# Adding four tiles' squares on VectorE at stage boundaries, with the weight split moved behind the residual in two parts

## The reference

```python
def rmsnorm(x, g):
    y = xf * lax.rsqrt(jnp.mean(xf * xf, axis=-1, keepdims=True) + RMS_EPS)
    return (y * g.astype(jnp.float32)).astype(x.dtype)
...
    m = c_act @ w + b
    shift, scale, gate = jnp.split(m, 3, axis=-1)
    h = rmsnorm(x, g) * (1.0 + scale[:, None, :]) + shift[:, None, :]
...
        x = x + 0.5 * g * swiglu(h, ffn_w_gate[i, 0], ffn_w_up[i, 0], ffn_w_down[i, 0])
```

## Time and profile before

| | |
|---|---|
| median of 3 runs | 1856.36 us (1854.56 to 1871.04) |
| the profiled execution | 1855.45 us, its span 1853.7 us |
| TensorE, weight loads, VectorE, ScalarE busy | 1765.2, 1711.8, 1440.4, 962.2 us |
| mean granted clock of TensorE | 0.98 |
| DMA | 426 MB moved, 230 GB/s on average |

### The profile page before, as it was taken

How to read it: one execution, slowest core, us unless ns; L and a number is a source line. 1 busy time by engine, 2 the same in 40 slices (tenths; PEclk the granted TensorE clock), 3 DMA queues, 4 the chain that set the end, 5 groups by cost and what they waited for, 6 DMA issues and landing times.

```text
span 1853.7 us, 34027 instructions
## 1 busy us (share of the span) xinstructions
PE 1765.2 (95%) x14590; PEld 1711.8 (92%) x14590; DVE 1440.4 (78%) x1714; ACT 962.2 (52%) x1257; POOL 0.2 (0%) x4
## 2 busy tenths in 40 slices
PE   5999999999999999999989999898999999989999
PEld 4999999998899999998979999897999988979999
DVE  7799988887799879986558998655888867457666
ACT  4434466666443453436564445556555555665553
POOL 0000000000000000000000000000000000000000
PEclk8999999999999999999999999999999998999999
DMA  9999834433698859883436987232487543325551
GB/s 396 417 376 370 325 114 160 160 137 137 225 387 350 322 213 406 334 324 132 164 114 263 379 356 286 113 135 102 171 291 250 195 164 136 132 71 182 181 190 37
DMA packets 68149, 426.23 MB, mean 230 GB/s; under 512 B 7488, under 2 KB 10832, under 8 KB 31824
## 3 DMA queue, kind: packets, MB, share of 16 engines
q1 hardware_dynamic: 63936, 416.22, 58.9%
q10 hardware_dynamic: 4112, 8.62, 1.4%
HBM read 423.74 MB, written 3.17 MB: 230 GB/s over the span
## 4 chain that ended last, share of the span: by engine, by line
PE 91%; DVE 3%; ACT 3%; DMA 2%; issue 1%; ACTq 0%; DVEq 0%; SPq 0%
PE bank L1447 26%; PE bank L1449 26%; PE bank L1448 26%; DMA mix<-mods 2%; PE bank L1513 2%; PE bank L1460 2%; PE bank L1462 1%; PE bank L1780 1%; PE bank L1467 1%; DVE w_lo L866 1%; PE bank L1622 1%; PE bank L1761 1%; PE bank L1657 0%; PE bank L1781 0%; PE bank L1714 0%
## 5 line engine op out<-in xcount | busy, mean ns | idle before, releaser
L1447 PE MATMUL bank<-h_hi,w_hi 128*128 128x256 f32 x2864 | 802.2, 280 | 4.2 <-DVE w_lo L866 3.6
L1449 PE MATMUL bank<-h_hi,w_lo 128*128 128x256 f32 x2864 | 796.9, 278 | 0.0
L1448 PE MATMUL bank<-h_lo,w_hi 128*128 128x256 f32 x2864 | 796.8, 278 | 0.0
L866 DVE TENSOR_TENSOR w_lo<-raw,w_hi 128x2048 fp32r<-128x2048 f32 x276 | 630.5, 2285 | 117.3 <-ACT w_hi L466 116.6
L466 ACT ACTIVATE w_hi<-raw 128x2048 fp32r<-128x2048 f32 x276 | 527.7, 1912 | 146.7 <-PE bank L1449 134.6
L1447 PEld LDWEIGHTS bank<-h_hi,w_hi 128*128 128x128 f32 x2864 | 540.2, 189 | 8.0 <-DVE w_lo L866 4.0
L1449 PEld LDWEIGHTS bank<-h_hi,w_lo 128*128 128x128 f32 x2864 | 542.1, 189 | 0.0
L1448 PEld LDWEIGHTS bank<-h_lo,w_hi 128*128 128x128 f32 x2864 | 539.3, 188 | 0.1
L1447 PE MATMUL bank<-a_hi,w_hi 128*128 128x256 f32 x1280 | 358.4, 280 | 2.1 <-DVE w_lo L866 2.1
L1448 PE MATMUL bank<-a_lo,w_hi 128*128 128x256 f32 x1280 | 355.5, 278 | 0.0
L1449 PE MATMUL bank<-a_hi,w_lo 128*128 128x256 f32 x1280 | 355.4, 278 | 0.0
(11 more groups left out here) (259 smaller groups left out, 1660.4 us busy)
## 6 DMA issues: line engine op xcount, KB each, us to landing
raw<-weights SPq DMA_DIRECT2D x276, 1024.0 KB, 4.9
modws<-mods SPq DMA_DIRECT2D x144, 768.0 KB, 6.9
mix<-mods SPq DMA_DIRECT2D x5, 1024.0 KB, 8.8
mix<-mods ACTq DMA_DIRECT2D x8, 512.0 KB, 12.8
biases<-scratch ACTq DMA_DIRECT2D x1, 2048.0 KB, 13.8
mix<-biases ACTq DMA_DIRECT2D x4, 512.0 KB, 3.8
modws<-mods SPq DMA_DIRECT2D x1, 1024.0 KB, 11.7
x<-xin SPq DMA_DIRECT2D x1, 1024.0 KB, 10.9
```

The source lines that it names most:

```text
L866: eng.tensor_tensor(w_lo[g % NW][:, :], raw[g % NRAW][:, :], w_hi[g % NW][:, :], ALU.subtract).then_inc(sems["wlo"], 1)
L1447: eng.matmul(dst, ah, bh, start=start, stop=False, skip_group_check=skip)
L1448: eng.matmul(dst, ah, bl, start=False, stop=False, skip_group_check=skip)
L1449: return eng.matmul(dst, al, bh, start=False, stop=stop, skip_group_check=skip)
```

## The change

At the boundaries that do not follow the mamba stage, VectorE adds the squares of tiles 0 to 3 into one tile with three additions (`add_squares`, counted in `sqa`), and TensorE sums five tiles instead of eight, all behind the fourth pair (`summed_squares`). In front of stage 6 it adds tiles 0 and 1, and 2 and 3, for both kinds of squares, and TensorE sums twelve tiles instead of sixteen. After the mamba stage the squares stay as they are.

The split that stood between VectorE's second and third pair is made in two parts (`late_split`): columns 0 to 1535 behind the last update, counted in a new semaphore `part`; columns 1536 to 2047 behind the `h_lo` tiles, counted in `wlo`. TensorE's second gemm of a stage waits for `part`, and for `wlo` at its seventh slice of the weights. This holds at all nine boundaries. In front of stage 6 ScalarE makes the square of `rstd` itself, as exponential of -1.0 times the logarithm, in place of VectorE's product.

```diff
@@ -174,6 +174,8 @@
         g = GROUPS[kind]
         out = {"fold": 4 if st else 0, "mods": 1, "modv": 1, "pair": 3, "xup": 8, "sq": 8, "ss": 1, "ln": 1, "rstd": 1,
                "t": 8, "hhi": 8, "hlo": 8, "ahi": 0, "alo": 0}
+        if st and self.stages[st - 1] != "mamba":
+            out |= {"sqa": 4 if st == RESCALED else 3}
...
@@ -485,8 +487,13 @@
                 if st == 0:
                     first_split()
                 k.wait("ss", st)
-                rs(rstd[:, :], bank[6][:, 0:T], 1.0 / D, eps_c, ("ln", "rstd"), st)
-                if final:
+                if not final:
+                    rs(rstd[:, :], bank[6][:, 0:T], 1.0 / D, eps_c, ("ln", "rstd"), st)
+                else:
+                    k.inc("ln", eng.activation(rstd[:, :], bank[6][:, 0:T], ACT.Ln, bias=eps_c, scale=1.0 / D))
+                    k.wait("ln", st)
+                    k.inc("ms2", eng.activation(rstd2, rstd[:, :], ACT.Exp, scale=-1.0))
+                    k.inc("rstd", eng.activation(rstd[:, :], rstd[:, :], ACT.Exp, scale=-0.5))
                     k.wait("ms2", st, b=1)
                     rs(rstd2, rstd2, 1.0 / D, eps_c, ("ln", "rstd"), st, b=1)
...
+            def late_split(st, part):
+
+                g, c = plan.first[st] + 1, (slice(0, 1536), slice(1536, 2048))[part]
+                eng.wait_ge(sems["whi"], g + 1)
+                eng.tensor_tensor(w_lo[g % NW][:, c], raw[g % NRAW][:, c], w_hi[g % NW][:, c],
+                                  ALU.subtract).then_inc(sems[("part", "wlo")[part]], 1)
...
@@ -963,10 +977,10 @@
 
             def norm(st):
                 final = st == RESCALED
-                k.wait("rstd", st)
                 r = rstd[:, :]
-                if final:
-                    k.inc("ms2", eng.tensor_tensor(rstd2, rstd[:, :], rstd[:, :], ALU.mult))
+                if not final:
+                    k.wait("rstd", st)
+                else:
                     k.wait("ms2", st)
                     k.inc("ms2", eng.tensor_tensor(rstd2, rstd2, bank[6][:, T:2 * T], ALU.mult))
                     k.inc("ms2", eng.tensor_tensor(gs[:, st, :], gs[:, st, :], par_("gfin"), ALU.mult))
...
@@ -985,6 +999,8 @@
                     k.inc("hlo", eng.scalar_tensor_tensor(
                         out=h_lo[:, m, :], in0=work3[:, m, :], scalar=modv[:, st, m:m + 1],
                         in1=h_hi[:, m, :], op0=ALU.add, op1=ALU.subtract))
+                if st:
+                    late_split(st, 1)
...
@@ -1005,14 +1021,29 @@
                 token = stages[st] == "mamba"
                 if token:
                     k.wait("rs2", st, b=1)
-                for pair in range(4):
-                    if pair == 2:
-                        split(st, b=NBLK[stages[st]] - 1)
-                    if pair < 3:
-                        k.wait("pair", st, b=pair)
+                nxt = st + 1
+                summed = nxt < NST and not token
+                final = nxt == RESCALED
+
+                def add_squares(m, other):
+                    for r in range(2 if final else 1):
+                        if other - m == 1:
+                            k.wait("sq", nxt, b=2 * other + r if final else other)
+                        else:
+                            k.wait("sqa", nxt, b=1)
+                        s = sq2 if r else work3
+                        k.inc("sqa", eng.tensor_tensor(s[:, m, :], s[:, m, :], s[:, other, :], ALU.add))
+
+                for two in ((0, 1), (2, 3), (4, 5), (6, 7)):
+                    if summed and two[0] == (6 if final else 4):
+                        add_squares(0, 1)
+                    if summed and two[0] == 6 and not final:
+                        add_squares(2, 3)
+                        add_squares(0, 2)
+                    if two[0] < 6:
+                        k.wait("pair", st, b=two[0] // 2)
                     else:
                         eng.wait_ge(sems["blk"], plan.first[st] + NBLK[stages[st]])
-                    two = (2 * pair, 2 * pair + 1)
                     if token:
                         for m in two:
...
@@ -1022,6 +1053,10 @@
                         k.inc("xup", eng.scalar_tensor_tensor(
                             out=x[:, m, :], in0=work3[:, m, :] if token else acc(m),
                             scalar=modv[:, st, 16 + m:17 + m], in1=x[:, m, :], op0=ALU.mult, op1=ALU.add))
+                if summed and final:
+                    add_squares(2, 3)
+                if nxt < NST:
+                    late_split(nxt, 0)
...
@@ -1438,7 +1473,10 @@
 
             def begin(st, i, a, b):
 
-                eng.wait_ge(sems["wlo"], k.block(st, i, a, b) + 1)
+                if st and isinstance(i, int) and i == 0 and b == 1:
+                    eng.wait_ge(sems["part"], st)
+                else:
+                    eng.wait_ge(sems["wlo"], k.block(st, i, a, b) + 1)
                 s = k.block(st, 0 if a % NW == 0 else i, a, b) % NW
                 return [w[s][:, :] for w in (w_hi, w_lo)]
 
@@ -1471,6 +1509,8 @@
                         if m and between:
                             between()
                         for kk in range(KT):
+                            if m == 0 and kk == 6 and st and isinstance(i, int) and i == 0 and b == 1:
+                                eng.wait_ge(sems["wlo"], k.block(st, b=1) + 1)
                             if tokens:
                                 mm = three(d, h_hi[:, kk, part], h_lo[:, kk, part], hi[:, kk, :], lo[:, kk, :],
                                            kk == 0, kk == KT - 1)
...
+
+            def summed_squares(st):
+
+                kinds = 2 if st == RESCALED else 1
+                order = [(0, 0), (2, 1), 4, 5, 6, 7] if kinds == 2 else [4, 5, (0, 2), 6, 7]
+                for n, what in enumerate(order):
+                    for r in range(kinds):
+                        if isinstance(what, tuple):
+                            m, b = what
+                            k.wait("sqa", st, b=2 * b + r if kinds == 2 else b)
+                        else:
+                            m = what
+                            k.wait("sq", st, b=2 * m + r if kinds == 2 else m)
+                        mm = eng.matmul(bank[6][:, r * T:(r + 1) * T], con_("ones"), (sq2 if r else work3)[:, m, :],
+                                        start=n == r == 0, stop=n == len(order) - 1, skip_group_check=True)
+                k.inc("ss", mm)
...
@@ -1568,19 +1624,21 @@
                                stop=True).then_inc(sems["gmods"], 1)
                 if more:
                     modulation(st + 1)
-                for pair in range(4):
-                    if pair == 3 and more:
+                token = stages[st] == "mamba"
+                for m in range(KT):
+                    if m == 6 and more and token:
                         squares(st + 1, 0)
-                    for m in (2 * pair, 2 * pair + 1):
-                        part = slice(m * P, (m + 1) * P)
-                        for kk in range(2):
-                            mm = three(acc(m), hi[:, kk, part], lo[:, kk, part], ahi[:, kk, :], alo[:, kk, :],
-                                       False, False, True)
-                    if pair < 3:
+                    part = slice(m * P, (m + 1) * P)
+                    for kk in range(2):
+                        mm = three(acc(m), hi[:, kk, part], lo[:, kk, part], ahi[:, kk, :], alo[:, kk, :],
+                                   False, False, True)
+                    if m in (1, 3, 5):
                         k.inc("pair", mm)
-                    else:
+                    elif m == 7:
                         mm.then_inc(sems["blk"], 1)
-                if more:
+                if more and not token:
+                    summed_squares(st + 1)
+                elif more:
                     squares(st + 1, 1)
                     squares(st + 1, 2)
                     squares(st + 1, 3)
```

More of the change, by code:

```diff
@@ L285, in sem @@
             return ctx.enter_context(nc.semaphore("s_" + name))
-        sems = {n: sem(n) for n in list(plan.total) + ["blk", "whi", "wlo", "macc", "const", "cact", "xst", "late", "mo", "go", "gmods", "half"]}
+        sems = {n: sem(n) for n in list(plan.total) + ["blk", "whi", "wlo", "macc", "const", "cact", "xst", "late", "mo", "go", "gmods", "half", "part"]}
         s_raw = [sem(f"raw{s}") for s in range(NRAW)]
```

## The result

| | before | after |
|---|---|---|
| median, 20 executions each | 1855.24 us (1840.77 to 1871.04) | 1842.56 us (1824.83 to 1851.63) |
| profiled execution | 1855.45 us | 1838.47 us |
| its span, mean granted clock | 1853.7 us, 0.982 | 1836.7 us, 0.987 |

The medians lie 12.7 us apart. The ratio over all executions is 0.9937, which is 11.7 us, with a 95% interval of 0.9916 to 0.9957, so the gain lies somewhere between 8 and 15.6. The 10.8 forecast (0.9942) lies inside.

The account below looks back on a forecast made before the run. TensorE was taken as the bound, with boundary costs reaching the end one for one; 7.6 (seven ordinary boundaries) + 1.8 (mamba) + 1.4 (stage 6) = 10.8 us off 1855.45 gives 1844.6, 1845.5 for a median; range 1839 to 1855.

Parts of the forecast that it names:

- 1.09 forecast: Ordinary boundary: fewer TensorE squares start the logarithm at 654.77 instead of 655.86; 1.09 us gained, 7.6 over seven boundaries.
- tile 6 0.21 late: Ordinary boundary: VectorE's additions make tile 6's update start at 652.62, 0.21 us later than the fourth pair allows.
- the upper bound of 1.30: Ordinary boundary: TensorE's own saving from three squares fewer, 3 x 0.433 = 1.30 us.
- The strict reading: VectorE's pipe empties after each operation before the next starts; gain 0.82 a boundary, 1.9 us less over seven.
- 1.80 forecast: After the mamba stage: with the split moved behind, the last pair's products start at 463.81 instead of 465.61; 1.80 us gained.
- 1.4 forecast: In front of stage 6: twelve squares instead of sixteen, 0.93, and ScalarE's Exp replacing VectorE's product, 0.46; bounds 0.46 and 2.2.
- The stop of 0.5 with a restart: In front of stage 6: TensorE does two squares, waits about 0.5 us, restarts (0.26) and does ten more.
- Spare 0.5 forecast: Split's first part on VectorE ends near 655.2, before normalised tiles need VectorE at 655.7; 0.5 us to spare, costing nothing.
- The rival of late loads: Raw buffer reloaded 10 us later, TensorE waits for each new stage's eighth block; 20 us slower, 1876; chance 0.05.
- squares that weren't the bound: Logarithm waits for something the shorter list doesn't shorten; only the mamba boundary and 0.46 are left, 1854; chance 0.09.
- additions that stay on the path: VectorE's additions stay on the path: ordinary boundaries gain only 0.40 us each, total 5.1, giving 1851; chance 0.18.
- The clock rival: First gemm after the gap at low clock, 1.43 us: all nine boundaries pay, 1848 (0.10); none pays, 1835 (0.03).

Follow-up runs that it names:

- e5: Changed kernel without the third addition: VectorE makes two sums, TensorE sums six tiles at an ordinary boundary; ratio to before 0.9964.
- e4: Changed kernel with the third addition behind the last updates, its sum taken last by TensorE, and another order in front of stage 6; ratio to before 0.9964.
- e9: The changed kernel measured once more, nothing altered, on one chip with e10; ratio to before 0.9887.
- e7: Changed kernel with the square of rstd back on VectorE, ScalarE's Exp removed; one execution, boundary in front of stage 6 16.35 us against 15.89.
- e6: Changed kernel with only TensorE's order in front of stage 6 altered, sum of tiles 2 and 3 behind tiles 4 and 5; ratio to before 0.9956.
- e8: e6 plus four unused float32 matmuls filling TensorE's idle stretch at each boundary (eight in front of stage 6); ratio to before 0.9972.
- e3: Changed kernel with the whole split in one piece behind the last update, no second part; ratio to before 0.9991.
- e10: The kernel of e8 measured once more, on the same chip as e9; ratio to before 0.9895.

## Why the prediction was right

**The ordinary boundary.** 1.09 forecast, 1.14 measured, and the mechanism held. The prediction let VectorE's additions decide: tile 6 0.21 late, the logarithm 2.15 us after the last updates begin. In the trace the updates begin at 649.20 and the logarithm at 651.35, 2.15 us as forecast. The chain gives that time to ten records of TensorE, as if they ran without a break. TensorE's weight loads show the break. Those of the squares after stage 2, then the same wait over the whole span (us in total, times, longest), then the loads of e5:

```profile
648.71 1.18 PEld L1570 LDWEIGHTS bank<-work,con 128*128 128x128 f32 x6
650.18 0.73 PEld L1570 LDWEIGHTS bank<-work,con 128*128 128x128 f32 x4 [0.29 <-ACT work L484]
```

```profile
PEld bank L1570 <- ACT work L484: 2.4, 7, 0.4
```

```profile
654.03 2.47 PEld L1569 LDWEIGHTS bank<-work,con 128*128 128x128 f32 x12
```

After tile 5 and the summed tile TensorE waits for ScalarE's square of tile 6, which in turn waited 0.77 for VectorE's update. It does so seven times, once at each ordinary boundary, and never at these boundaries in e5. So with three additions VectorE decides, and with two TensorE does. The updates begin 0.21 after the pair's end; some 0.05 of that is the passing on from TensorE to VectorE (in e5 the pair ends at 654.31 and the updates begin at 654.35), so the lateness costs 0.16 of the upper bound of 1.30, where the forecast had 0.21. That is the whole difference between 1.09 and 1.14. The expectations of e4 and e5 took TensorE's ten records for the bound and were mistaken in that.

**The drain.** The strict reading of the Trainium skill (page "VectorE: DVE Perf Modes", section "The DRAIN you can't avoid") would have given 0.82. A pair of updates takes 0.79 from start to start, 0.395 each, where one alone takes 0.48, so these overlap. The trace goes with the remark in the same section of the Trainium skill that an operation that isn't held starts earlier.

**After the mamba stage.** 1.80 forecast, 1.26 in one profile and 1.73 in the other. The timeline after the mamba stage, TensorE, VectorE and ScalarE, against the earlier trace rows:

```profile
462.09 2.98 PE L1553 MATMUL bank<-work,con 128*128 128x256 f32 x12
...
462.29 0.75 DVE L1049 TENSOR_TENSOR work<-bank,mix 128x256 f32<-128x256 f32 x2 [0.48 <-PE bank L1487]
...
465.11 0.47 ACT L472 ACTIVATE rstd<-bank,small 128x256 f32<-128x256 f32 x1 [0.83 <-PE bank L1553]
```

From the fourth pair's end to the logarithm it is 3.02 us (3.01 in e9), where the earlier trace rows have 468.42 - 463.76 = 4.66 and the forecast 2.86: 1.64 gained. The 0.16 that is missing is the start of VectorE's products, 0.20 after the pair's end and not 0.05. What varies lies ahead. From the modulation to the fourth pair's end, in before, in the changed kernel, and in e9:

```profile
456.31:463.76 7.45, 7.45 (x55) 7.34 (x54) 5.86 (x16) 4.38 (x8) 0.00 (x0) 0.88 0.00 1
```

```profile
454.27:462.09 7.82, 7.82 (x55) 7.71 (x54) 5.58 (x19) 5.40 (x10) 0.00 (x0) 0.83 0.00 1
```

```profile
454.76:462.12 7.36, 7.36 (x56) 7.25 (x55) 5.58 (x19) 4.91 (x10) 0.00 (x0) 0.89 0.00 1
```

The lengths follow the granted clock: at 0.83 it is 0.37 more than before, and 1.64 - 0.37 leaves the 1.26; at 0.89 it is 0.09 less, and leaves the 1.73. What the first profile lacks is clock, not work.

**In front of stage 6.** 1.4 forecast (0.93 + 0.46), 1.58 measured, and 1.44 in e9. e7 gives the Exp its 0.46; the squares gave 1.12 (0.98 in e9). The stop of 0.5 with a restart was a gap of 0.32, and e6 shows that another order avoids it.

**The split in two parts.** Spare 0.5 forecast, 0.57 measured. 1.75 and 0.69 forecast, and measured (group of L880: shortest, median, longest in ns):

```profile
L880 DVE TENSOR_TENSOR w_lo<-raw,w_hi x18: 677/1215/1751, 226.2 to 1651.7; 128x1536 fp32r<-128x1536 f32 x9, 128x512 fp32r<-128x512 f32 x9
```

TensorE waits for neither part at any boundary, and the loads issued later cost next to nothing: beside the five waits in stage 0 there is one of 1.0 at its end and one of 1.2 ahead of the residual of stage 7, where before had 0.9. The rival of late loads falls with that; the rivals of squares that weren't the bound and of additions that stay on the path (0.40 a boundary) fall with the 1.14. The clock rival was right that the idle stretch brings it, and that its coming isn't settled by the stretch alone: seven of nine before, five and three after, with the same wait.

**Luck.** The three terms were 7.6, 1.8 and 1.4, and 7.95, 1.26 and 1.58 were measured; that their sums agree at 10.8 is luck. The totals cannot tell 10.8 from 8 or 15, and both sets of runs of the changed kernel gained more than its boundaries did; it is the lengths of the boundaries that bear the forecast out.

## What to carry to other kernels

Where two engines share a boundary, lightening one pays only as far as the other lets it: here the moved split was worth nothing, the additions cost 0.8, and both gained 1.1. Place a sum where the engine that uses it would otherwise wait. Judge changes of a few tenths by the length of the place itself in the trace; it repeats to 0.2 us where the total wanders by ten.

## What the runs showed of the hardware

At a granted clock of 1.00, with TensorE busy throughout, the step from one matmul to the next has two lengths. Three stretches of 140 us inside feed-forward stages 5, 7 and 9, before and then after:

```profile
1000.00:1140.00 140.00, 140.00 (x1237) 140.00 (x1237) 129.60 (x80) 58.33 (x44) 0.00 (x0) 1.00 0.91 363
1330.00:1470.00 140.00, 140.00 (x1191) 140.00 (x1190) 124.76 (x128) 73.18 (x76) 0.00 (x0) 1.00 0.73 260
1680.00:1820.00 140.00, 140.00 (x1191) 140.00 (x1190) 98.27 (x111) 74.74 (x77) 0.00 (x0) 1.00 0.49 173
```

```profile
1000.00:1140.00 140.00, 140.00 (x1191) 140.00 (x1190) 125.68 (x78) 56.49 (x42) 0.00 (x0) 1.00 0.90 349
1330.00:1470.00 140.00, 140.00 (x1237) 140.00 (x1237) 129.56 (x131) 75.17 (x77) 0.00 (x0) 1.00 0.72 257
1680.00:1820.00 140.00, 140.00 (x1192) 140.00 (x1191) 95.74 (x109) 73.25 (x76) 0.00 (x0) 1.00 0.43 150
```

1237 matmuls are a step of 0.113 us, 1191 one of 0.118; no other was read in the feed-forward stages of the twelve profiles (0, 2, 3, 5, 7 and 9). DMA traffic doesn't decide it: the longer step stands at 349 GB/s and at 150, the shorter at 363 and 257. Stages 2, 3, 5, 7 and 9 keep their step almost from the start; in stage 0 it changed on the way in three profiles (e5, e7, e8), each time where the granted clock was below 1. Which stage has which differs between executions of the same code: stages 5 and 9 in the first profile of the changed kernel, 3 and 7 in e9. A stage at the longer step takes some 6.5 us more. One to five of the six stages are at it in the twelve profiles, stage 0 of those three not counted (e8 five, e6 four, e3 three, before two). Outside the boundaries the twelve spans run from 1729 to 1754 us; less 6.6 us for each such stage, from 1716 to 1728. So this is the larger part of the scatter of these spans, and why the profiled executions of e3, e6 and e8 gained less than their boundaries did. That it moves the medians in the same way is likely, but each median rests mostly on executions without a profile.

What draws the step was not found, but one thing goes with it. Of the sixty stages 2, 3, 5, 7 and 9 of the twelve profiles, 28 began with a first product at the low clock, and 3 of these ran at the longer step; of the 32 that began at the high clock, 24 did. Keeping the clock up at a boundary saves 1.5 us; if it brings the longer step, that costs 6.5. e8 (five of five at the longer step) looks like such a trade, e10 (two of five) less so, and no run here separates the two.
